# Conditioning vectors 2 to 8 from VectorE row products, and another ScalarE order in the first attention

## The chip, the cores and the metric

One core of a Trainium2 chip runs the whole program. The metric is the device time of one execution in microseconds. Engines are named as in the profile: PE is TensorE (PEld its weight loads), DVE VectorE, ACT ScalarE, POOL GpSimd, SP SyncE, which here only issues DMAs.

## What is computed

A conditioned block over 256 tokens of width 1024 with 256 context tokens (a feed-forward half, a token mixer with a long convolution and a differential attention, a second feed-forward half), followed by a second block with a recurrent mixer and a 16-expert layer. All is float32. The change concerns the nine conditioning vectors, for the token stream and the context stream, and the first attention:

```python
mod_x = split((silu(c)     @ w_ada + b_ada), 9)     # w_ada: 1024 x 9216
mod_c = split((silu(c_ctx) @ w_ada + b_ada), 9)
xs = ffn_half(xs, mod_x[0], mod_x[1], mod_x[2], g[0], g[1], w_ff_in, w_ff_out)   # shift, scale, gate
cs = ffn_half(cs, mod_c[0], mod_c[1], mod_c[2], g[0], g[1], w_ff_in, w_ff_out)
hx = modulate(rmsnorm(xs, g[2]), mod_x[3], mod_x[4])
hc = modulate(rmsnorm(cs, g[2]), mod_c[3], mod_c[4])
# mixer; xs += mod_x[5] * ...; second half uses mod_x[6], mod_x[7], mod_x[8]
# attention, for each of 8 heads and two maps m:
#   p = softmax(q k^T / 8);  p = p[0] - lam * p[1];  o = p @ v
```

## The kernel before

All activations lie transposed, features on the 128 partitions, tokens along the free axis. One SBUF tensor, `arena`, is cut by hand into 23 pages of 2048 words, whose use changes from stage to stage. Weights stream through four pages, the ring: SyncE loads slabs of 1 MB (16 blocks of 128x128) in the order in which TensorE uses them, a new one as soon as TensorE has started on the slab behind (`slab_started`). The order of the work on each engine is written out by hand; engines meet through semaphores, `full[b]` and `evac[b]` for the eight PSUM banks.

The conditioning vectors: `cond_s` holds silu of both conditioning vectors, two used columns in each 32. `ada_sums` (matmul at L768) multiplies one slab of `w_ada` (256 input rows by 1024 outputs) with them in four groups of 32 columns of the array, four slabs for each conditioning vector; VectorE copies the result (L1827), `ada_columns` (L782) turns it with four small matmuls, and VectorE adds the bias (L1832) into `mods`. Vectors 0 and 1 are made at the start (`ada_head`). Vectors 2 to 6 are made in ffn1_in, the first feed-forward product: its loop has 5 turns of 4 quarters, each with one slab of `w_ada` and then a pair of output tiles (gate and up, 8 products of 128x128 by 512 tokens each). ScalarE applies Silu to the gate tile (L1475), VectorE multiplies by the up tile (L1863). Vectors 7 and 8 are made between the tiles of z (24 tiles of 8 products by 256 tokens; ScalarE L1503, VectorE L1894 and L1896).

The start: ScalarE squares the tokens, takes the root (L1432), and issues 8 DMAs (L1447 to L1454). VectorE takes the reciprocal, then `normalise` (L1777, L1783) writes the input of ffn1_in, one of 8 feature tiles after the other, and TensorE's first product waits for each.

The end of ffn1_in: `filter_in_time` makes 8 tiles of the convolution filter on four banks (TensorE L818), VectorE multiplies them with the decay (L1855), ScalarE takes magnitudes (L1461), TensorE sums them (L825), and ffn1_out follows.

The first attention, for each head hd: TensorE makes the scores of the next head (L948, banks 0 to 3), part of another projection (L954), the transposes of this head's probabilities (L977, banks 5 and 6), more of L954, and the value product (L986, bank 7). VectorE takes maxima (L1953), normalises and mixes the two maps (L1961 to L1968), and copies bank 6 (L1974). ScalarE takes the exponentials of the next head from banks 0 to 3 (L1531), then copies bank 5 (L1538), then bank 7 (L1541).

Of the kernel before, what the change touches and what calls it, by code (L numbers as in the profile page):

```python
# [16 lines left out]
P = 128  # L17
D = 1024
T = 256
# [9 lines left out]
RING = 4  # L29
EX_RING = 16  # L30
# [24 lines left out]
DENSE = [("ffn1_in", FT + 20), ("ffn1_out", 11), ("z", 12 + 8), ("qk", 8), ("v", 4), ("gates", 8),  # L55
# [5 lines left out]
def _rot(n, banks=(0, 1, 2, 3)):  # L61
# [4 lines left out]
          ("ada_head", {7: 2, 6: 2}), ("ffn1_in", {0: 11, 1: 11, 2: 11, 3: 11, 7: 5, 6: 5}),  # L66
          ("w4", _rot(8)), ("knorm", {5: 1}), ("ffn1_out", _rot(8)),
          ("kdft", _rot(10)), ("z", {**_rot(24), 7: 2, 6: 2}), ("qk", {**_rot(16), 5: 8, 6: 8}), ("ut", {5: 2, 6: 2}), ("v", _rot(12)),
# [132 lines left out]
def cols(v):  # L201
    return v.reshape(-1, P).T
# [6 lines left out]
def lay_out(inp):  # L209
    g = {k: np.asarray(v) for k, v in inp.items()}  # L210
    ada = np.stack([k_pairs(g["w_ada"][0][:, m * D:m * D + D]) for m in range(N_MOD)])
# [6 lines left out]
    mixed = []  # L218
    for i in range(5):
        for q in range(4):  # L220
            mixed += [ada[2 + i][q:q + 1], slabs(f1[4 * i + q:4 * i + q + 1])]
    mixed += [slabs(f1[20:22])]
    w_in = g["w_in"][0]
    zs, late = slabs(blocks(w_in[:, :3 * D])), np.concatenate([ada[7], ada[8]])
    z = [a[i:i + 1] for i in range(12) for a in (zs, late) if i < len(a)]
# [12 lines left out]
        *mixed, slabs(blocks(g["w_ff_out"][0, 0])), *z, slabs(blocks(w_in[:, 3 * D:5 * D])),  # L238
# [12 lines left out]
    cond = np.stack([cols(g["c"][0]), cols(g["c_ctx"])], axis=2).reshape(P, KD * 2)  # L251

# [24 lines left out]
    out = {"ada_head": np.concatenate([ada[0], ada[1]]), "dense": dense, "experts": experts, "tokens": tokens, "cond": cond, "cols": cc, "filt": filt,  # L277
# [5 lines left out]
_ARRAYS = ["ada_head", "dense", "experts", "tokens", "cond", "cols", "filt", "w4", "lora", "router", "zT", "decay", "Fu", "FK", "FKalt",  # L283
# [4 lines left out]
def build(nc, dram, out_dram):  # L288
# [8 lines left out]
    with ctx:  # L297
# [19 lines left out]
        ring_flat = [page(i, SLAB) for i in range(RING)]  # L317
        head_flat = [page(i, SLAB) for i in (6, 7, 8, 9, 10, 11, 12, 14)]
# [17 lines left out]
        gain = sb("gain", [P, 4 * KD])  # L336
        filt = page(20, 3 * 64)[0:64]
# [162 lines left out]
        cond_ready = sem("cond_ready")  # L500
        sq_ready = sem("sq_ready")
# [216 lines left out]
        def _(pe):  # L718
# [30 lines left out]
            def tiles(stage, count, k_tiles, rhs, n=T, after=None, norm=None):  # L749

                for t in range(count):
# [3 lines left out]
                    if after:  # L755
                        after(t)

            def ada_sums(stage, k, kp):
# [4 lines left out]
                if head and kp == 0:  # L763
                    pe.wait_ge(head_in[k], 64)
# [1565 lines left out]
```

## Time and profile before

| | us |
|---|---|
| median of 3 runs | 2259.53 |
| lowest and highest | 2257.13, 2260.47 |
| the profiled execution | 2257.64 |
| its span | 2255.8 |
| TensorE busy in the span | 1975.7 |
| VectorE busy | 466.9 |
| ScalarE busy | 293.7 |
| TensorE's mean granted clock, share of full | 0.923 |

The page of the profile gives busy times by engine, the span in 40 slices, the chain of work that ended last, and the costliest groups of instructions. The trace behind it was asked for tables by stretch and for the instructions in order of time, one engine after the other, around each place that the change touches.

### The profile page before, as it was taken

How to read it: one execution, taken by the hardware profiler on the slowest of the kernel's cores; microseconds unless marked ns; L12 is line 12 of the kernel's file. 1: busy time of each engine (PE TensorE's matmuls, PEld its weight loads, DVE VectorE, ACT ScalarE, POOL GpSimd, SP SyncE). 2: the span in 40 equal slices, each digit the busy share in tenths (PEclk: the TensorE clock that was granted, in tenths of full speed). 3: DMA queues.
4: the chain of work that ended last, by engine and by line, in shares of the span. 5: the costliest groups of instructions: out<-in, count | busy, mean ns of one | idle time of the engine just before them, and what ended most of it. 6: DMA issues, size and time to landing. Idle time of an engine off the chain costs nothing.

```text
span 2255.8 us, 24413 instructions
## 1 busy us (share of the span) xinstructions
PE 1975.7 (88%) x10258; PEld 1253.2 (56%) x10258; DVE 466.9 (21%) x918; ACT 293.7 (13%) x590; POOL 37.7 (2%) x32
## 2 busy tenths in 40 slices
PE   5999999999999999989899989799999756565665
PEld 2444445444578478668688867688678512121212
DVE  4000001001422221351300023724142300000001
ACT  2000001001211001330110013312131100000001
POOL 0000000000000000000000000212000000000000
PEclk9999999999999999999899999889799887877878
DMA  9333331221263112203344423100034899999996
GB/s 365 118 143 149 142 121 72 75 75 56 89 247 131 67 64 94 94 38 131 139 157 149 149 101 123 57 3 3 19 112 160 338 422 421 422 421 422 421 422 253
DMA packets 55883, 393.95 MB, mean 175 GB/s; under 512 B 6355, under 2 KB 6708, under 8 KB 8892
## 3 DMA queue, kind: packets, MB, share of 16 engines
q1 hardware_dynamic: 54000, 384.29, 43.2%
q10 hardware_dynamic: 1804, 8.47, 1.0%
q8 instruction: 65, 1.06, 0.2%
q14 instruction: 14, 0.11, 0.0%
HBM read 391.69 MB, written 1.05 MB: 174 GB/s over the span
## 4 chain that ended last, share of the span: by engine, by line
PE 31%; DMA 17%; DVE 3%; issue 1%; SPq 1%; ACT 1%; POOL 0%; ACTq 0%; DVEq 0%; POOLq 0%
PE bank L729 20%; DMA arena<-experts_dram 17%; PE bank L1098 3%; PE bank L1340 2%; SPq L671 1%; PE bank L740 1%; PE bank L1167 1%; DVE arena L2106 1%; PE bank L1184 1%; PE bank L1182 1%; DVE rstd L1749 0%; PE bank L1170 0%; PE bank L1223 0%; PE bank L1270 0%; PE bank L1198 0%
## 5 line engine op out<-in xcount | busy, mean ns | idle before, releaser
L729 PE MATMUL bank<-arena 128*128 128x256 f32 (+1 forms) x4096 | 1168.1, 446 | 12.6 <-issue 5.0
L729 PEld LDWEIGHTS bank<-arena 128*128 128x128 f32 x4096 | 783.0, 192 | 392.3 <-issue 307.1
L1340 PE MATMUL bank<-arena 128*32 128x512 f32 x1536 | 246.9, 803 | 170.2 <-DMA arena<-experts_dram 170.2
L1340 PEld LDWEIGHTS bank<-arena 128*32 128x32 f32 x1536 | 66.2, 141 | 345.4 <-issue 345.3
L1863 DVE TENSOR_TENSOR arena<-sil,bank 128x512 f32 (+3 forms) x44 | 24.4, 555 | 445.7 <-PE bank L729 445.7
L1475 ACT ACTIVATE sil<-bank 128x512 f32<-128x512 f32 (+1 forms) x44 | 21.6, 491 | 413.8 <-PE bank L729 413.7
L1098 PE MATMUL bank<-arena 64*64 64x64 f32 x2048 | 65.9, 227 | 6.8 <-POOL arena L700 5.5
L1098 PEld LDWEIGHTS bank<-arena 64*64 64x64 f32 x2048 | 65.0, 143 | 8.1 <-POOL arena L700 5.8
L2290 DVE TENSOR_TENSOR arena<-arena,bank 128x512 f32<-128x512 f32 x8 | 5.5, 688 | 258.8 <-PE bank L1340 258.8
L910 PE MATMUL bank<-arena 128*128 128x256 f32 x256 | 55.6, 379 | 0.0
L910 PEld LDWEIGHTS bank<-arena 128*128 128x128 f32 x256 | 48.6, 190 | 7.0 <-issue 0.5
L1428 ACT ACTIVATE sq<-bank 128x256 f32<-128x256 f32 (+1 forms) x24 | 10.9, 455 | 296.5 <-PE bank L729 296.5
L740 PE MATMUL bank<-sq,small 128*128 128x256 f32 (+1 forms) x96 | 37.8, 541 | 10.4 <-ACT sq L1428 9.6
L1758 DVE TENSOR_TENSOR rstd<-rstd,sq 128x256 f32<-128x256 f32 (+1 forms) x18 | 9.3, 514 | 181.5 <-ACT sq L1428 181.5
L768 PE MATMUL bank<-arena,cond_s 128*32 128x512 f32 x288 | 40.0, 645 | 1.3 <-issue 1.3
L1719 ACT ACTIVATE arena<-bank 128x512 f32<-128x512 f32 x8 | 4.8, 597 | 234.6 <-PE bank L1340 234.6
L834 PE MATMUL bank<-arena 128*128 128x512 f32 x80 | 34.7, 592 | 0.0
L2129 DVE TENSOR_TENSOR arena<-arena,bank 128x512 f32<-128x512 f32 x40 | 27.5, 688 | 32.6 <-PE bank L1098 29.6
L740 PEld LDWEIGHTS bank<-sq,small 128*128 128x128 f32 x96 | 17.7, 221 | 29.4 <-ACT sq L1428 26.4
L1428 ACT ACTIVATE sq<-arena 128x256 f32<-128x256 f32 (+1 forms) x48 | 23.1, 487 | 80.7 <-PE bank L740 38.9
L2296 DVE COPY arena<-bank 128x512 f32<-128x512 f32 x4 | 2.8, 692 | 147.7 <-PE bank L1340 147.7
L954 PE MATMUL bank<-arena 128*128 128x256 f32 x128 | 33.2, 405 | 0.0
(310 smaller groups left out, 1311.4 us busy)
## 6 DMA issues: line engine op xcount, KB each, us to landing
arena<-experts_dram SPq DMA_DIRECT2D x189, 1024.0 KB, 22.7
arena<-dense_dram SPq DMA_DIRECT2D x165, 1024.0 KB, 4.8
arena<-ada_head_dram SPq DMA_DIRECT2D x8, 1024.0 KB, 18.4
arena<-experts_dram SPq DMA_DIRECT2D x6, 512.0 KB, 7.2
arena<-tokens_dram ACTq DMA_DIRECT2D x1, 2048.0 KB, 11.4
arena<-masks_dram ACTq DMA_DIRECT2D x1, 1184.0 KB, 5.9
arena<-decay_dram ACTq DMA_DIRECT2D x1, 1024.0 KB, 9.6
arena<-FK_dram ACTq DMA_DIRECT2D x1, 1024.0 KB, 10.2
```

The costliest lines, as they stand in the source:

```text
L671: sp.dma_start(ex_flat[j], slab).then_inc(ex_loaded[j], 16)
L729: ins = mm(out, lhsT=w, rhs=rhs(k), start=k == 0, stop=k == k_tiles - 1)
L740: mm(ps[4][:, 0:n], lhsT=ones, rhs=sq_v[:, j % 2, 0:n], start=j == 0, stop=j == 7)\
L768: ins = mm(ps[7][32 * q_:32 * q_ + 32, :], lhsT=cond_v[:, 2 * kp + par, :], rhs=slab[:, par * D + half * 512:par * D + half * 512 + 512], ...
L834: ins = mm(ps[n % 4][:, :], lhsT=part, rhs=hfil[:, kt, (n % 2) * 512:(n % 2) * 512 + 512], start=kt == 0, stop=kt == 3)
L910: ins = mm(ps[tt][:, 0:256], lhsT=h1[:, k, tt * P:tt * P + P], rhs=ring_wide[slot][:, k, :], start=k == 0, stop=k == KD - 1)
L954: ins = mm(ps[4][:, 0:T], lhsT=w, rhs=hy[:, k, :], start=k == 0, stop=k == KD - 1)
L1098: ins = mm(out[r64, H * hd:H * hd + H], lhsT=lhs[r64, 8 * d + hd, :], rhs=eye2[r64, :] if rhs is None else rhs[r64, 8 * d + hd, :], start= ...
L1340: ins = mm(ps[banks[half]][32 * e:32 * e + 32, :], lhsT=lhs[:, 2 * kp + par, CAP * e:CAP * e + CAP], rhs=slab[e][par][:, half * 512:half * ...
L1428: A(sq_v[:, j % 2, 0:n], src, ACT.Square).then_inc(sq_ready, 1)
L1863: tt_(hid[:, at, 0:n], sil_v[:, q_ % 2:q_ % 2 + 1, 0:n], ps[b + 1][:, 0:n].unsqueeze(1), mult)\
L2129: tt_(dst, dst, ps[b][:, :].rearrange("p (i n) -> p i n", n=H), sub).then_inc(evac[b], 1)
```

## The change

Only vectors 0 and 1 are still made by TensorE. For vectors 2 to 8, the weights are laid out transposed, as 56 tiles of 128 outputs (partitions) by 1024 inputs, 0.5 MB each, in a ring of five buffers of their own. Both conditioning vectors are loaded spread over all partitions (`cond_wide`, 128x2048, 1 MB) and go through one Silu on ScalarE. For each tile VectorE does two `scalar_tensor_tensor` with a sum along the free axis, one for each stream, into a column of `ada_acc`; after ten tiles it adds the bias into `mods`. The tiles are placed behind VectorE's gating products in ffn1_in, 2, 2, 3 and 3 in the quarters of a loop turn and three behind each of the last two. ScalarE issues the reloads, each after a wait for the tile that used the buffer. Its DMAs for `cond_wide` and the first five tiles stand ahead of the 8 that it issues at the start, and VectorE waits for the Silu before its first normalisation. Slabs of `w_ada` leave SyncE's stream in ffn1_in and z.

In the attention ScalarE takes the exponentials of banks 0 and 1 of the next head, copies bank 5, and then takes those of banks 2 and 3.

```diff
+ADA_TILES = (N_MOD - N_HEAD_MODS) * KD
+ADA_RING = 5
+ADA_SHARE = (2, 2, 3, 3)
...
+    ada_rest = w_ada[:, N_HEAD_MODS * D:].T.reshape(ADA_TILES, P, D)
+    cond_wide = np.broadcast_to(np.concatenate([g["c"][0], g["c_ctx"]])[None, :], (P, 2 * D))
...
+        ada_ring = [page(at, D) for at in (15, 15.5, 21, 21.5, 18)]
+        cond_wide = page(20, 2 * D)
...
                 with pe.Fori(0, 5) as i:
-                    st.loop(i, per)
+                    st.loop(i, 4)
                     for q_ in range(4):
-                        if with_ada:
-                            ada_sums(stage + "_in", i, q_)
                         pair(q_, i * 2 + q_ // 2)
-                    if with_ada:
-                        ada_columns(stage + "_in", i, i)
...
-            tiles("z", 24, KD, lambda k: h1[:, k, 0:T], T, late_ada, 1)
+            tiles("z", 24, KD, lambda k: h1[:, k, 0:T], T, norm=1)
...
             root(0, 512)
+            act.dma_start(cond_wide, dram["cond_wide"]).then_inc(cond_wide_in, 16)
+            for s in range(ADA_RING):
+                act.dma_start(ada_ring[s], dram["ada_rest"][s]).then_inc(ada_in[s], 16)
             act.dma_start(w4[0:64, :], dram["w4"]).then_inc(decay_in, 16)
...
                 with act.Fori(0, 5) as i:
                     for q_ in range(4):
                         gate(q_, i * 2 + q_ // 2)
+                        if ada:
+                            for t in range(sum(ADA_SHARE[:q_]), sum(ADA_SHARE[:q_ + 1])):
+                                act.wait_ge(ada_used, i * 11 + (t + 2))
+                                act.dma_start(ada_ring[t % ADA_RING],
+                                              dram["ada_rest"][ds(i * 10 + (t + ADA_RING), 1), :, :].rearrange("s p n -> (s p) n"))\
+                                    .then_inc(ada_in[t % ADA_RING], 16)
...
+            act.wait_ge(cond_wide_in, 16)
+            A(cond_wide, cond_wide, ACT.Silu).then_inc(cond_wide_ready, 1)
+            ffn("ffn1", 1, y1, 512, magnitudes, ada=True)
...
-            exps(0)
+            exps(0, range(4))
             for hd in range(HEADS):
                 if hd + 1 < HEADS:
-                    exps(hd + 1)
+                    exps(hd + 1, range(2))
                 got(act, "att", 5, hd)
                 A(pT[:, 4 * (hd % 2):4 * (hd % 2) + 4, 0:P], ps[5][:, :].rearrange("p (k n) -> p k n", n=P), ACT.Copy)\
                     .then_inc(evac[5], 1)
+                if hd + 1 < HEADS:
+                    exps(hd + 1, range(2, 4))
...
+            dve.wait_ge(cond_wide_ready, 1)
+            V.memset(ada_acc[:, :], 0.0).then_inc(ada_used, 1)
             normalise(X, h1, [(0, T, gain_v[:, 0, :], mod(0, 0)), (T, 2 * T, gain_v[:, 1, :], mod(0, 1))])
...
+                def ada_tile(t, i):
+                    w = ada_ring[t % ADA_RING]
+                    dve.wait_ge(ada_in[t % ADA_RING], i * 32 + 16 * (t // ADA_RING + 1))
+                    dve.wait_ge(ada_used, i * 11 + (t + 1))
+                    stt(sq[:, :], w, 1.0, cond_wide[:, 0:D], mult, mult, accum_out=ada_acc[:, 2 * t:2 * t + 1])
+                    stt(w, w, 1.0, cond_wide[:, D:2 * D], mult, mult, accum_out=ada_acc[:, 2 * t + 1:2 * t + 2])                        .then_inc(ada_used, 1)
...
-                        if with_ada and q_ == 3:
-                            ada_sums(stage + "_in", i)
                         up(q_, i * 2 + q_ // 2, ds(i * 4 + q_, 1))
+                        if with_ada:
+                            for t in range(sum(ADA_SHARE[:q_]), sum(ADA_SHARE[:q_ + 1])):
+                                ada_tile(t, i)
...
+                for q_ in range(2):
+                    up(q_, 10, slice(20 + q_, 21 + q_))
+                    if with_ada:
+                        for t in range(3 * q_, 3 * q_ + 3):
+                            ada_tile(t, 5)
```

## Rows read from the trace of the kernel before

**Rows 1.** The page: busy time by engine, and the chain's engines.
```profile
PE 1975.7 (88%) x10258; PEld 1253.2 (56%) x10258; DVE 466.9 (21%) x918; ACT 293.7 (13%) x590; POOL 37.7 (2%) x32
...
PE 31%; DMA 17%; DVE 3%; issue 1%; SPq 1%; ACT 1%; POOL 0%; ACTq 0%; DVEq 0%; POOLq 0%
```
**Rows 2.** Busy time by stretch: PE, PEld, DVE, ACT, POOL, clock, DMA share, GB/s.
```profile
1750.00:2000.00 250.00, 161.62 (x995) 69.01 (x994) 28.61 (x65) 16.87 (x29) 0.00 (x0) 0.80 0.97 403
```
**Rows 3.** In order of time, ffn1_in: start, duration, engine, line, operation.
```profile
63.60 1.06 PE L768 MATMUL bank<-arena,cond_s 128*32 128x512 f32 x8
...
336.96 0.19 PEld L729 LDWEIGHTS bank<-arena 128*128 128x128 f32 x1 [0.24 <-issue]
...
349.40 0.19 PEld L729 LDWEIGHTS bank<-arena 128*128 128x128 f32 x1 [0.24 <-issue]
...
378.71 7.13 PE L818 MATMUL bank<-arena,fh 64*128 64x512 f32 x16
```
**Rows 4.** In order of time, z: TensorE's first and nineteenth tile, ScalarE at one.
```profile
597.95 7.07 PE L729 MATMUL bank<-arena 128*128 128x256 f32 x32
...
671.36 23.99 PE L729 MATMUL bank<-arena 128*128 128x256 f32 x110
...
682.01 0.56 ACT L1503 ACTIVATE arena<-bank,col_sb 128x256 f32<-128x256 f32 x1 [2.89 <-PE bank L729]
```
**Rows 5.** VectorE's groups by form (count, busy us, mean ns), and an accumulator read.
```profile
L1968 DVE SCALAR_TENSOR_TENSOR arena<-arena,tiny 128x512 f32<-128x512 f32 x16 | 11.3, 748 | 0.3
...
L2045 DVE TENSOR_TENSOR arena<-arena 128x1024 f32<-128x1024 f32 x2 | 2.5, 1226 | 0.1
...
1782.64 0.07 DVE L2251 DVE_READ_ACCUMULATOR sq<-fh,sil 16x1 f32 x1
```
**Rows 6.** The start in order of time; clock by stretch; a DMA to landing; a group.
```profile
6.45 9.29 SPq L639 DMA_DIRECT2D arena<-dense_dram  x4
...
36.99 0.48 ACTq L1447 DMA_DIRECT2D arena<-w_dram  x1
...
43.27 1.28 ACT L1475 ACT_TABLE_LOAD   x1 [4.36 <-issue]
...
44.66 0.49 DVE L1777 SCALAR_TENSOR_TENSOR arena<-arena,gain,rstd 128x256 f32<-128x256 f32 x1
...
50.00:51.00 1.00, 1.00 (x2) 0.50 1.04 395
...
arena<-decay_dram ACTq DMA_DIRECT2D x1, 1024.0 KB, 9.6
...
L1697 ACT ACTIVATE arena<-arena 128x2048 f32<-128x2048 f32 x2 | 3.7, 1902 | 0.0
```
**Rows 7.** The end of ffn1_in in order of time, and the clock by stretch.
```profile
378.89 0.69 DVE L1863 TENSOR_TENSOR arena<-sil,bank 128x512 f32<-128x512 f32 x1 [13.04 <-PE bank L729]
379.94 1.48 DVE L1855 TENSOR_TENSOR arena<-bank,arena 128x512 f32<-128x512 f32 x2 [0.36 <-PE bank L818]
...
387.29 12.29 PE L825 MATMUL bank<-small,arena 128*128 128x1 f32 x64 [1.45 <-ACT arena L1461]
...
390.00:392.00 2.00, 2.00 (x11) 2.00 (x11) 0.00 (x0) 0.00 (x0) 0.00 (x0) 0.50 0.00 0
```
**Rows 8.** The first attention in order of time, VectorE, ScalarE and TensorE.
```profile
943.83 2.50 DVE L1953 TENSOR_REDUCE tiny<-bank 128x1 f32<-128x512 f32 x4
...
949.49 0.18 DVE L1961 RECIPROCAL tiny<-tiny 128x4 f32<-128x4 f32 x1
...
952.98 0.69 DVE L1953 TENSOR_REDUCE tiny<-bank 128x1 f32<-128x512 f32 x1 [0.82 <-PE bank L948]
...
949.90 1.99 PE L986 MATMUL bank<-arena 128*128 128x256 f32 x8 [0.96 <-ACT arena L1538]
...
955.97 0.69 ACT L1531 ACTIVATE arena<-bank,tiny 128x512 f32<-128x512 f32 x1 [3.20 <-DVE tiny L1955]
...
959.29 1.99 PE L986 MATMUL bank<-arena 128*128 128x256 f32 x8 [0.96 <-ACT arena L1538]
```

More of the change, by code:

```diff
@@ L52 @@
 N_COLS = _at
-DENSE = [("ffn1_in", FT + 20), ("ffn1_out", 11), ("z", 12 + 8), ("qk", 8), ("v", 4), ("gates", 8),
+DENSE = [("ffn1_in", FT), ("ffn1_out", 11), ("z", 12), ("qk", 8), ("v", 4), ("gates", 8),
          ("hyout", 4), ("daout", 4), ("wo", 4), ("ffn2_in", FT), ("ffn2_out", 11), ("rwkv", 18.5 + 8)]
@@ L210, in lay_out @@
     g = {k: np.asarray(v) for k, v in inp.items()}
-    ada = np.stack([k_pairs(g["w_ada"][0][:, m * D:m * D + D]) for m in range(N_MOD)])
+    w_ada = g["w_ada"][0]
+    ada = np.concatenate([k_pairs(w_ada[:, m * D:m * D + D]) for m in range(N_HEAD_MODS)])
+    ada_rest = w_ada[:, N_HEAD_MODS * D:].T.reshape(ADA_TILES, P, D)
     def ffn_in(w):
@@ L280, in lay_out @@
     return {k: np.ascontiguousarray(v) for k, v in out.items()}
-_ARRAYS = ["ada_head", "dense", "experts", "tokens", "cond", "cols", "filt", "w4", "lora", "router", "zT", "decay", "Fu", "FK", "FKalt",
+_ARRAYS = ["ada_head", "ada_rest", "cond_wide", "dense", "experts", "tokens", "cond", "cols", "filt", "w4", "lora", "router", "zT", "decay", "Fu", "FK", "FKalt",
            "Finv", "rope", "small", "headbc", "masks"]
@@ L500, in build @@
         cond_ready = sem("cond_ready")
+        cond_wide_in = sem("cond_wide_in")
+        cond_wide_ready = sem("cond_wide_ready")
+        ada_in = [sem(f"ada_in{i}") for i in range(ADA_RING)]
+        ada_used = sem("ada_used")
         sq_ready = sem("sq_ready")
@@ L747, in stat_of_sum, with tiles @@
                 mm(ps[4][:, 0:n], lhsT=ones, rhs=rstd[:, 0:n], start=True, stop=True).then_inc(full[4], 1)
-            def tiles(stage, count, k_tiles, rhs, n=T, after=None, norm=None):
+            def tiles(stage, count, k_tiles, rhs, n=T, norm=None):
                 for t in range(count):
@@ L761, in ada_sums @@
                     take(pe, stage, 7, k)
-                head = stage == "ada_head"
-                if head and kp == 0:
+                if kp == 0:
                     pe.wait_ge(head_in[k], 64)
-                slab = head_flat[4 * k + kp] if head else st.whole(ring_flat)
+                slab = head_flat[4 * k + kp]
                 for q_ in range(4):
@@ L770, in ada_sums @@
                              start=kp == 0, stop=kp == KD // 2 - 1)
-                    if q_ == 0 and not head:
-                        ins.then_inc(slab_started, 1)
                 if kp == KD // 2 - 1:
@@ L836, in filter_spectrum, with ffn @@
                     ins.then_inc(full[n % 4], 1)
-            def ffn(stage, r, src, hid, n, with_ada, norm, between=None):
+            def ffn(stage, r, src, hid, n, norm, between=None):
                 def pair(q_, use):
@@ L1467, in filter_spectrum, with ffn @@
                         .then_inc(evac[n % 4], 1)
-            def ffn(stage, r, y, n, between=None):
+            def ffn(stage, r, y, n, between=None, ada=False):
                 def gate(q_, use):
@@ L1880, in _ @@
             V.reciprocal(tiny[:, 8:16], tiny[:, 8:16]).then_inc(kn_ready, 1)
-            evacuated(dve, "ffn1_in", 6, 4)
+            dve.wait_ge(ada_used, 63)
             for r in range(2):
```

56 lines of the change are left out of this document (24 added, 32 removed).

## The prediction

> **What bounds the kernel now.** I began with the page's busy times and its chain [rows 1]. The reader is to see a TensorE at work for 88% of the span, and a chain that consists of TensorE and, at the end, of expert loads. The table by stretches shows where each limit holds: the last 500 us move 403 GB/s with TensorE at 161.6 of 250 us [rows 2], so there loads set the pace. They are only issued behind events of the stages before them, so what those stages gain shifts the whole tail forward and is kept. Before 1000 us TensorE is the limit nearly everywhere, above all in the first feed-forward block and in the z projection, and TensorE work removed there counts in full. Three places are different: the start, where VectorE's normalisation releases TensorE; the filter made in time at the end of ffn1_in, where VectorE, ScalarE and TensorE take turns; and the first attention, where a loop of VectorE, ScalarE and TensorE turns more slowly than TensorE's own work.
>
> **Part 1: TensorE loses 28 conditioning slabs and 7 transpositions.**
> In ffn1_in the slab of quarter (0, 1) starts at 63.60, and the stage's successor (L818) starts at 378.71 [rows 3]: 315.1 us for 21 pairs of tiles, 19 slabs and 5 groups of L782. A pair is 32 weight loads (16 products, two records each). Between 336.96 and 349.40 there are 29 steps of load to load [rows 3], 0.429 us each, so a pair alone is 13.73 us and 21 pairs are 288.3. The difference is 26.8 us; the twentieth slab, at 44 us, fills a hole in which TensorE waits for VectorE anyway and gives nothing. VectorE sat idle for 13 us between two gating products here (its idle time before L1863 [rows 7]), and ScalarE likewise, so nothing else is late next: **-26.8**.
> In z, the first tile starts at 597.95 and the nineteenth at 671.36 [rows 4]: 73.4 us for 18 tiles, 8 slabs, 2 groups of L782. ScalarE's step at each tile (0.56 busy, 2.89 idle) shows a tile alone at 3.45 us [rows 4]; 18 are 62.1. VectorE's two or three steps of 0.5 us fit under that, so TensorE stays the limit. **-11.3**.
> The bytes of weights are the same as before. They move from SyncE's queue, at 1 MB, to ScalarE's, at 0.5 MB, and those of z now come in ffn1_in: 50 MB in some 300 us, 170 GB/s, against the 403 that the tail shows [rows 2]. A tile's next load is asked for five tiles before its use, some 27 us. I cost this at nothing.
>
> **Part 2: the row products on VectorE.** 56 tiles, two scalar-tensor-tensor with sum each, of 128x1024. The nearest rows: the same instruction on 512 elements from SBUF takes 0.748 us (two in a row 1.41), a plain tensor-tensor of 1024 takes 1.226, and an accumulator read is 0.07 [rows 5]. So 1.23 + 0.07 = 1.3 each, 2.6 a tile, 146 us in all; bounds are 1.23 and 1.50 (twice the 0.748) + 0.07 each. I take 1.3, since two rows at a distance of a factor of two agree on one element per cycle. A quarter with three tiles is 7.9 us and the gating product 0.7, against 13.7 us of TensorE work: hidden. ScalarE now waits for those tiles before it issues their reloads, and its next Silu is queued behind; it comes about 9.4 us after the last one instead of 6.9, but the bank that it frees is wanted only at 13.7. Hidden too.
> The Trainium skill (Vector Engine (DVE) Microarchitecture Reference, Points that are easy to get wrong) says that this very instruction halves its throughput when both sources are SBUF tensors other than bf16, which is what the change uses. The trace's 0.748 us for 512 such elements [rows 5] is not half speed beside 1.226 for 1024 of a tensor-tensor, so the row speaks against it; the row has no accumulator, though, and I keep the case as a rival.
>
> **Part 3: the start.** VectorE now waits, before its first normalisation, for ScalarE's Silu over the broadcast conditioning vector. Ahead of that Silu on ScalarE's queue are now 14 DMA issues instead of 8. The 8 begin at 36.99 and the table load behind them at 43.27 [rows 6]: 0.78 each. Six more at this mean are 4.7 us, so the table load starts at 48.0. Then 1.28 for it and 1.90 for 2048 elements (the same length at L1697 [rows 6]): 51.1. The load of 1 MB itself was issued first and should be down by 46 or so: the decay, issued second at the same place and of the same size, took 9.6 us [rows 6] behind 0.5 MB. VectorE's first step moves from 44.66 [rows 6] to about 51.2 with the memset: 6.5 us later, and TensorE with it. Bounds: 0.48 an issue, as the first of them [rows 6], +4.7; or a queue that is held as SyncE's was, four issues in 9.29 us [rows 6], for the last four, +13. TensorE's granted clock was at half (0.50, 1.2 GHz) until 51 [rows 6], after it had stood and waited for VectorE; now it stands longer and will again be at half when the products begin, with VectorE's pace of 1.31 us a product hiding most of it. I add 0.5: **+7.0**.
>
> **Part 4: the end of ffn1_in.** VectorE has three tiles and a bias left after its last gating product, before it takes over filter tiles. Now: gating product at 378.89, filter products from 379.94, column sums of the magnitudes at 387.29 [rows 7]. New, with T = 378.71: gating product done at T + 0.9, tiles until T + 8.8, bias T + 9.1. TensorE has filled four banks by T + 3.5 and stands for 6.4 us. Then the other four at 0.86 us each as now: column sums from T + 14.9 instead of T + 8.6, +6.3. But a stop of 1.45 us already ends in a half clock here (0.50 in 390 to 392 [rows 7]), and 6.4 us of idling will do so earlier: the four matmuls at 1.71 instead of 0.86 add 3.4, and the first sums, now still at full clock, 0.7. **+10.4**, with bounds +6.3 (no fall of the clock) and +14 (the half clock reaches on into ffn1_out).
>
> **Part 5: ScalarE's order in the attention.** In the steady state a head takes 9.40 us (TensorE's L986 waits for ScalarE's copy and starts at 959.29, as at 949.90) [rows 8]. VectorE starts at 949.49, its reductions start only at 952.98, after 0.82 us of waiting for scores (so it was done with the rest at 952.16, 2.67 later); ScalarE's exponentials start at 955.97, the copy of bank 5 behind them is what the value product waits for [rows 8]. Four exponentials and a copy of 0.6 thus fill the 3.3 us from 955.97 to 959.29, 0.67 an exponential. With the new order the copy stands between the second and third exponential: the copy and with it the value product and the next scores come 1.3 us sooner, the last exponentials 0.6 later. The loop is then VectorE 2.67, four reductions back to back 2.50 (as at 943.83 [rows 8]), 0.25, four exponentials and the copy 3.3, and 0.2: about 8.95 instead of 9.40. Over 5 such heads that is 2.2; the change costs 0.6 once at the first of them and saves 1.6 behind the last, where the transposes come sooner. **-3.2**, bounds 0 (the loop closes over another engine at 9.4) and -4.5.
>
> **Sum:** -26.8 - 11.3 - 3.2 + 7.0 + 10.4 = -23.9. The profiled execution took 2257.64 us (span 2255.8), so 2233.7; the median of the runs is 2259.53, so about 2235.5. I say 2235.
>
> **Rivals.**
> (a) *The sum makes a row product twice as long* as the tensor-tensor of the same size: 2.46 and the read, 5.0 a tile. Ten tiles and four gatings are 53 us against 54.9 of a loop turn, so the loop stays hidden, but a quarter with three tiles takes 15.7 against 13.7 and VectorE comes about 6 us late to the last gating product; then three tiles take 15 instead of 7.9. Together 13 more: 2248. For it: no row here has a sum over 1024 elements and two tensors. Against: the accumulator read of 0.07 and the 0.748 [rows 5]. This is the case that the page's rule above describes.
> (b) *ScalarE's queue is held at the start*: +13 instead of +7, 2241. For it: SyncE's four issues at 2.3 us each behind 11 others [rows 6], and ScalarE's own mean of 0.78 against 0.48 for its first. Against: SyncE's eight before them were short.
> (c) *The clock doesn't fall in the new hole, or the start is cheaper than I hold*: 2229.
> (d) *VectorE becomes the bound of ffn1_in*. A loop turn of TensorE is 54.9; VectorE needs 10 tiles and 3.0. It decides above 5.19 us a tile. Beyond that each microsecond of a tile costs 50 + 3 us, and the whole change turns to a loss at 5.5 us a tile; with 6 us (3 us an instruction) it gives about 2286. For it: 112 long instructions put on one engine, with DMA-filled buffers. Against: it wants over twice the longest of rows 5.
> (e) *The change doesn't do what it says*: reloads by ScalarE arrive late, since each is queued behind gatings and waits for VectorE, and VectorE stands at an empty buffer with the gating queued behind it. It has 27 us for half the size of a transfer that took 9.6 among full queues [rows 6]; at 5 us in each loop turn the gain would be gone: 2260.
>
> **How the numbers follow.** Forecast 0.60, for which its own range is 2229 to 2242; (a) 0.10, (b) 0.12, (c) 0.12, (d) 0.02, (e) 0.04. The range of 8 in 10 takes in (a), (b) and (c) with the bounds of parts 3 to 5: down to 2228 (start +4.7, end +6.3, attention -4.5) and up to 2248 (start +13, end +14, attention 0), the lower end widened by 2 us for what separates executions of one kernel (2257.1 to 2260.5). Within 0.2% (4.5 us), about what a measurement can tell from no change, means over 2255; only (e) in a milder form reaches that: same 0.03. Slower is (d) and the worst of (e): 0.03. Faster 0.94.
>
> **What would show each step.** Right: no gap for slabs in L729's run in ffn1_in, a pair each 13.7 us; the VectorE instruction at 1.3 us; the first normalisation at 51; a hole of 6 us in L818 and the clock at 0.50 behind it; heads at 8.95. Wrong: VectorE idle on ada_rest loads; pairs longer than 13.8; the Silu of 2048 after 54; the clock at full through L818; heads still at 9.4. The prediction as a whole is wrong if TensorE waits for a bank inside ffn1_in.

## The result, and the profile of the changed kernel

| | before | changed |
|---|---|---|
| median of 4 runs, us | 2259.46 | 2226.84 |
| lowest and highest | 2257.13, 2260.47 | 2225.04, 2228.48 |
| the profiled execution | 2257.64 | 2228.48 |
| its span | 2255.8 | 2226.7 |
| TensorE's mean granted clock | 0.923 | 0.919 |

The ratio is 0.9857, with an interval of 0.984 to 0.9874: 32.6 us less in the medians, 29.1 less in the two spans. 2235 was forecast, with 2226 to 2248 as the range. The two differences are not the same because the profiled execution of the changed kernel lies 1.6 above its median, and that of the kernel before 1.8 below its own.

The changed kernel's page, busy times, and from its list of groups and of DMA issues the new work (count, busy us, mean ns; for a DMA, size and us to landing); the first line answers to [rows 1]:

```profile
PE 1939.1 (87%) x9978; PEld 1244.4 (56%) x9978; DVE 592.0 (27%) x1135; ACT 290.4 (13%) x587; POOL 37.7 (2%) x32
...
L1877 DVE SCALAR_TENSOR_TENSOR sq<-arena 128x1024 f32<-128x1024 f32 x56 | 68.4, 1222 | 1.5
L1878 DVE SCALAR_TENSOR_TENSOR arena<-arena 128x1024 f32<-128x1024 f32 x56 | 68.3, 1220 | 0.0
...
arena<-ada_rest_dram ACTq DMA_DIRECT2D x56, 512.0 KB, 3.7
```

TensorE has 280 matmul records fewer (each product leaves two), VectorE 125 us more work. A row product takes 1.22 us.

The start in order of time (start, duration, engine, line, operation, idle before and what ended it), which answers to [rows 6]:

```profile
35.55 0.33 ACTq L1437 DMA_DIRECT2D arena<-cond_wide_dram  x1
...
44.96 1.11 ACTq L1447 DMA_DIRECT2D router<-router_dram  x1
46.10 1.28 ACT L1496 ACT_TABLE_LOAD   x1 [8.62 <-issue]
47.39 1.91 ACT L1496 ACTIVATE arena<-arena 128x2048 f32<-128x2048 f32 x1
49.36 0.46 DVE L1783 SCALAR_TENSOR_TENSOR arena<-arena,gain,rstd 128x256 f32<-128x256 f32 x1 [5.91 <-issue]
...
51.78 7.52 PE L736 MATMUL bank<-arena 128*128 128x512 f32 x12 [8.82 <-DVE arena L1789]
```

The Silu stands behind 14 DMA issues and its table load, and VectorE behind the Silu for 5.91 us.

The end of ffn1_in, in order of time and by stretch (TensorE busy, granted clock, DMA share, GB/s), which answers to [rows 3] and [rows 7]:

```profile
356.67 3.70 PE L820 MATMUL bank<-arena,fh 64*128 64x512 f32 x8
356.85 0.69 DVE L1871 TENSOR_TENSOR arena<-sil,bank 128x512 f32<-128x512 f32 x1 [5.79 <-PE bank L736]
357.45 1.22 DVE L1877 SCALAR_TENSOR_TENSOR sq<-arena 128x1024 f32<-128x1024 f32 x1
358.60 0.08 DVE L1877 DVE_READ_ACCUMULATOR sq<-arena 128x1 f32 x1
...
364.92 2.48 DVE L1863 TENSOR_TENSOR arena<-bank,arena 128x512 f32<-128x512 f32 x4
...
365.65 7.19 PE L820 MATMUL bank<-arena,fh 64*128 64x512 f32 x8 [5.29 <-DVE arena L1863]
...
374.29 11.04 PE L827 MATMUL bank<-small,arena 128*128 128x1 f32 x51 [1.44 <-ACT arena L1454]
...
362.00:364.00 2.00, 0.00 (x0) 0.78 0.00 0
364.00:366.00 2.00, 0.34 (x1) 0.50 0.00 0
...
388.00:392.00 4.00, 4.00 (x6) 0.50 0.19 33
```

Here T of the prediction is 356.67. TensorE fills its banks in 3.70 us, stands 5.29 us until VectorE is through the three tiles behind its last gating product, and does the other half at half clock (granted 0.50, 1.2 GHz), which still holds at 392.

The first attention, the value products of two heads in a row, which answers to [rows 8]:

```profile
943.34 0.59 ACT L1542 ACTIVATE arena<-bank 128x512 f32<-128x512 f32 x1
943.99 1.99 PE L976 MATMUL bank<-arena 128*128 128x256 f32 x8 [0.27 <-ACT arena L1542]
...
952.70 1.99 PE L976 MATMUL bank<-arena 128*128 128x256 f32 x8 [0.27 <-ACT arena L1542]
```

A head now takes 952.70 - 943.99 = 8.71 us, before 9.40.

**Where the 29.1 us come from**, by the starts of TensorE's stages in the two traces (of the start, VectorE's first normalisation):

| stretch | before | changed | difference | forecast |
|---|---|---|---|---|
| until the first normalisation | 44.66 | 49.36 | +4.7 | +7.0, with the clock |
| from there to the first filter product | 334.05 | 307.31 | -26.7 | -26.8 |
| to the column sums | 8.58 | 17.62 | +9.0 | +9.7 |
| to the start of z | 210.66 | 213.51 | +2.9 | +0.7 |
| z, to the first scores | 325.93 | 314.59 | -11.3 | -11.3 |
| attention, to the sums behind its heads | 81.97 | 76.91 | -5.1 | -3.2 |
| everything behind it | 1249.95 | 1247.4 | -2.6 | 0 |
| sum | | | -29.1 | -23.9 |

### The profile page after: what moved, and what is told of

Its sections match the earlier page's. It is cut to its first block, busy times and chain, and to the rows that moved or that the text cites. A ratio compares the mean times of both kernels' runs of the same rounds, so it can differ in the third digit from the quotient of the medians.

```text
span 2226.7 us, 24201 instructions
## 1 busy us (share of the span) xinstructions
PE 1939.1 (87%) x9978; PEld 1244.4 (56%) x9978; DVE 592.0 (27%) x1135; ACT 290.4 (13%) x587; POOL 37.7 (2%) x32
## 4 chain that ended last, share of the span: by engine, by line
PE 31%; DMA 17%; DVE 3%; issue 1%; ACT 1%; SPq 1%; POOL 0%; ACTq 0%; DVEq 0%; POOLq 0%
PE bank L736 21%; DMA arena<-experts_dram 17%; PE bank L1088 3%; PE bank L1330 2%; SPq L678 1%; PE bank L747 1%; PE bank L1157 1%; DVE arena L2130 1%; PE bank L1174 1%; PE bank L1172 1%; DVE rstd L1755 0%; PE bank L1160 0%; PE bank L1213 0%; PE bank L1260 0%; PE bank L1188 0%
## 5 line engine op out<-in xcount | busy, mean ns | idle before, releaser
L1330 PE MATMUL bank<-arena 128*32 128x512 f32 x1536 | 247.1, 804 | 170.2 <-DMA arena<-experts_dram 170.2
L1330 PEld LDWEIGHTS bank<-arena 128*32 128x32 f32 x1536 | 66.3, 141 | 344.9 <-issue 344.8
L1088 PE MATMUL bank<-arena 64*64 64x64 f32 x2048 | 66.0, 227 | 6.7 <-POOL arena L707 5.5
L1088 PEld LDWEIGHTS bank<-arena 64*64 64x64 f32 x2048 | 65.2, 143 | 8.1 <-POOL arena L707 5.8
L1877 DVE SCALAR_TENSOR_TENSOR sq<-arena 128x1024 f32<-128x1024 f32 x56 | 68.4, 1222 | 1.5
L1878 DVE SCALAR_TENSOR_TENSOR arena<-arena 128x1024 f32<-128x1024 f32 x56 | 68.3, 1220 | 0.0
L900 PE MATMUL bank<-arena 128*128 128x256 f32 x256 | 55.6, 379 | 0.0
L747 PE MATMUL bank<-sq,small 128*128 128x256 f32 (+1 forms) x96 | 37.5, 535 | 10.4 <-ACT sq L1418 9.6
L1977 DVE TENSOR_REDUCE tiny<-bank 128x1 f32<-128x512 f32 x32 | 19.9, 680 | 53.1 <-PE bank L938 53.1
## 6 DMA issues: line engine op xcount, KB each, us to landing
arena<-tokens_dram ACTq DMA_DIRECT2D x1, 2048.0 KB, 12.2
```

The lines of the kernel that those rows point to most:

```text
L747: mm(ps[4][:, 0:n], lhsT=ones, rhs=sq_v[:, j % 2, 0:n], start=j == 0, stop=j == 7)\
L900: ins = mm(ps[tt][:, 0:256], lhsT=h1[:, k, tt * P:tt * P + P], rhs=ring_wide[slot][:, k, :], start=k == 0, stop=k == KD - 1)
L1088: ins = mm(out[r64, H * hd:H * hd + H], lhsT=lhs[r64, 8 * d + hd, :], rhs=eye2[r64, :] if rhs is None else rhs[r64, 8 * d + hd, :], start= ...
L1330: ins = mm(ps[banks[half]][32 * e:32 * e + 32, :], lhsT=lhs[:, 2 * kp + par, CAP * e:CAP * e + CAP], rhs=slab[e][par][:, half * 512:half * ...
L1877: stt(sq[:, :], w, 1.0, cond_wide[:, 0:D], mult, mult, accum_out=ada_acc[:, 2 * t:2 * t + 1])
L1878: stt(w, w, 1.0, cond_wide[:, D:2 * D], mult, mult, accum_out=ada_acc[:, 2 * t + 1:2 * t + 2]) .then_inc(ada_used, 1)
```

## The experiments

The table shows what differs, not that the causes add up as I read them. My theory, A, is that the start, the hole at the end of ffn1_in and the attention each have the price or gain that the table shows, one by one and in sum, and that the row products themselves and their 28 MB of loads are hidden. The rival, B, stands in each expectation: in the main, that a gain would be given back later, or that the row products cost something even where no gap shows them. All ratios are to the kernel before, run on the same chip.

### The wait for the Silu put behind the normalisation

```diff
-            dve.wait_ge(cond_wide_ready, 1)
-            V.memset(ada_acc[:, :], 0.0).then_inc(ada_used, 1)
             normalise(X, h1, ...)
+            dve.wait_ge(cond_wide_ready, 1)
+            V.memset(ada_acc[:, :], 0.0).then_inc(ada_used, 1)
```

> The changed kernel (2226.8 us) with VectorE's wait for the Silu and the memset moved behind the first normalisation; nothing is left out. Theory A: the wait is what moved the first normalisation from 43.4 (gain ready) to 49.36, so it starts at 43.5, TensorE's first product likewise 5.9 us sooner, and the kernel takes about 2221. Theory B: TensorE is at half clock there and the DMA engines are full, so most of the 6 us is lost again in the first products: 2225 or more.

2224.04 us (five runs, 2218.57 to 2227.73), ratio 0.9852 (0.9838 to 0.9866), span 2216.7. In order of time, the start, the end of ffn1_in and z:

```profile
44.01 1.67 DVE L1783 SCALAR_TENSOR_TENSOR arena<-arena,gain,rstd 128x256 f32<-128x256 f32 x4
...
46.45 7.55 PE L736 MATMUL bank<-arena 128*128 128x512 f32 x12 [2.97 <-DVE arena L1789]
...
582.57 77.65 PE L736 MATMUL bank<-arena 128*128 128x256 f32 x359
```

The first product is 5.3 us earlier than the changed kernel's 51.78, and z as much (582.57 against 587.80): nothing of it is given back in the first 580 us. But the medians differ by 2.8 us only, and this kernel's runs lie 9 us apart, into the changed kernel's. Its median lies between the 2221 of A and the 2225 of B, so by time alone this run doesn't tell one from the other; the third experiment does.

### The last six tiles ahead of the last gating product

```diff
-for q_ in range(2):
-    up(q_, 10, slice(20 + q_, 21 + q_))
-    for t in range(3 * q_, 3 * q_ + 3):
-        ada_tile(t, 5)
+for t in range(2):
+    ada_tile(t, 5)
+up(0, 10, slice(20, 21))
+for t in range(2, 6):
+    ada_tile(t, 5)
+up(1, 10, slice(21, 22))
```

Two tiles now come ahead of the gating product (0, 10), and the other four behind it, so that none is left behind the last one.

> The changed kernel with the last six tiles placed two before the gating product of pair 20 and four behind it, none behind that of pair 21; nothing is left out. Theory A: the three tiles behind the last gating product make the hole of 5.3 us in L820 and with it the early half clock; both go, the column sums start 8.6 us behind L820 instead of 17.6 and ffn1_out loses the 2.8 us that it gained in length: 12 less, 2215. Theory B: only VectorE's share of the hole goes (6.3 us) and the granted clock falls as early as it does now: 2220.

2214.64 us (2213.21 to 2218.82), ratio 0.9807 (0.9793 to 0.982), span 2217.0: 12.2 us less than the changed kernel. TensorE in order of time:

```profile
356.48 7.13 PE L820 MATMUL bank<-arena,fh 64*128 64x512 f32 x16
...
365.05 11.91 PE L827 MATMUL bank<-small,arena 128*128 128x1 f32 x64 [1.44 <-ACT arena L1454]
...
575.74 84.55 PE L736 MATMUL bank<-arena 128*128 128x256 f32 x391
```

The eight filter products (16 records) are one run of 7.13 us again, as in [rows 3], and the column sums come 8.57 us behind its start (before 8.58, changed 17.62). z starts 12.1 us sooner than in the changed kernel: 9.0 for the hole and the four products at half clock, 2.8 for the half clock that reaches on behind it (column sums to z 210.7 against 213.5), 0.2 from before it. So the order of six tiles is worth 12 us in this comparison, more than the 10.4 of my sum; the next experiment gives a second one, and it is smaller.

### Both

> Both moves together. Theory A: the two places are far apart and add up: 2226.8 - 5.9 - 11.9 = 2209. Theory B: they share something (the clock, the loads): over 2212.

2209.83 us (2208.83 to 2212.36), ratio 0.979 (0.9776 to 0.9803), span 2208.0. It leaves nothing out and is the fastest version that was run, 17.0 us below the changed kernel (14.8 below its repetition, further down). Against the second experiment, in the same batch, the later wait gives 4.8 us, where A says 5.9, with ranges that don't touch (2208.83 to 2212.36 against 2213.21 to 2218.82): the start's price is real, and the runs of the first experiment were too scattered to show it. The column sums:

```profile
359.45 13.72 PE L827 MATMUL bank<-small,arena 128*128 128x1 f32 x64 [1.45 <-ACT arena L1454]
```

The two places are not quite independent, and what B names, the clock, is what they share. There is no hole here, and yet the column sums take 13.72 us, at half clock from their start (0.53 in the first 2 us, then 0.50) and as long as behind the hole (13.81 in full), where the tiles early alone had 11.91 and the kernel before 12.29. So the filter products start 5.6 us sooner than with the tiles early alone, but z only 4.0. Measured against the kernel with the later wait, the tiles' order brings z forward by 10.8 us, of which 0.5 come from before the filter products: 10.3, and not 12.

### No row products at all

This kernel leaves out the conditioning vectors 2 to 8 (they are zero): no loads of their weights or of `cond_wide`, no Silu over it, no tiles.

```diff
-act.dma_start(cond_wide, dram["cond_wide"]).then_inc(cond_wide_in, 16)
-for s in range(ADA_RING):
-    act.dma_start(ada_ring[s], dram["ada_rest"][s]).then_inc(ada_in[s], 16)
...
-dve.wait_ge(cond_wide_ready, 1)
-V.memset(ada_acc[:, :], 0.0).then_inc(ada_used, 1)
+V.memset(mods[:, 4 * KD:], 0.0).then_inc(ada_used, 1)
...
-ffn_in("ffn1", hid1, 512, True)
+ffn_in("ffn1", hid1, 512, False)
```

> The changed kernel without the row products, their loads, the wide Silu and the waits: vectors 2 to 8 are zeros, so that part of the computation is left out. It shows what the row products cost wherever they lie. Theory A: all that they cost is the start (5.9) and the end of ffn1_in (11.9), so this takes 2209, the same as both moves together within 2 us. Theory B: the 137 us of VectorE work and 28 MB of loads in ffn1_in also slow TensorE's products or loads while hidden: clearly below 2206, and below both moves together.

2209.21 us (2208.25 to 2217.75), ratio 0.9793 (0.9776 to 0.981), span 2207.5. Its filter products and z, and behind the dots the same two lines of the kernel with both edits:

```profile
351.04 7.13 PE L820 MATMUL bank<-arena,fh 64*128 64x512 f32 x16
...
571.61 88.66 PE L736 MATMUL bank<-arena 128*128 128x256 f32 x410
```

```profile
350.88 7.13 PE L820 MATMUL bank<-arena,fh 64*128 64x512 f32 x16
...
571.75 88.44 PE L736 MATMUL bank<-arena 128*128 128x256 f32 x409
```

They agree within 0.2 us at both places, and the medians within 0.6. So 137 us of VectorE work and 28 MB of loads cost nothing that can be measured, once the wait at the start and the tail are out of the way. What the change pays, some 15 us against its repetition and 17 against its first runs, is paid at those two places.

### The attention's order alone

```diff
-def exps(hd):
+def exps(hd, banks):
-    for b in range(4):
+    for b in banks:
...
-    exps(hd + 1)
+    exps(hd + 1, range(2))
...
+if hd + 1 < HEADS:
+    exps(hd + 1, range(2, 4))
```

> The kernel before with ScalarE's new order in the attention and nothing else changed. Theory A, from the trace of the changed kernel (heads at 8.71 us, 5.05 less between the first scores and the head sums): 5 less than before, 2252 to 2254, ratio 0.9978. Theory B, the sum of the prediction: 3.2 less, ratio 0.9986. Theory C: part of the 5 us came from the clock's phase, which the other edits shifted: 0 to 2 less.

On the kernel before, with nothing else changed: 2252.95 us (2249.63 to 2257.34), ratio 0.998 (0.9971 to 0.9989), span 2252.0; the kernel before had 2257.2 beside it. TensorE in order of time, a value product and the sums behind the heads:

```profile
982.55 1.99 PE L986 MATMUL bank<-arena 128*128 128x256 f32 x8 [0.28 <-ACT arena L1538]
...
991.26 1.99 PE L986 MATMUL bank<-arena 128*128 128x256 f32 x8 [0.27 <-ACT arena L1538]
...
1000.45 3.62 PE L993 MATMUL bank<-arena,small 128*8 128x256 f32 x16 [0.92 <-ACT arena L1545]
```

The heads are 8.71 us here too. From the first scores (922.75) to the sums are 77.70 us, where before had 81.97: 4.3 us, and 4.3 in the medians. The new order is worth 4.3 here, more than my 3.2. In the ten traces that have the other edits too the same stretch takes 75.8 to 76.9 us, up to 1.9 less than here; what makes that difference was not taken apart.

### Each row product done twice

```diff
 stt(sq[:, :], w, 1.0, cond_wide[:, 0:D], ...)
+stt(sq[:, :], w, 1.0, cond_wide[:, 0:D], ...)
+stt(sq[:, :], w, 1.0, cond_wide[:, D:2 * D], ...)
 stt(w, w, 1.0, cond_wide[:, D:2 * D], ...)
```

A wait of VectorE's for itself stands between two of them. This is rival (a)'s tile, made real: the prediction said that the loop would stay hidden up to 5.19 us a tile.

> The changed kernel with each row product made twice, each waiting for the one before; results are the same. It doubles the hidden work. Theory A: a tile takes 5.2 us; a quarter with three tiles then needs 16.3 us against 13.7, VectorE comes some 7 us late to the last gating product and spends 8 more behind it, while within the loop TensorE never waits for a bank: 15 to 16 more, 2243. Theory B: the cover is thinner than thought, TensorE waits for banks in each loop turn: over 2260. Theory C: VectorE's work is no part of the price: 2227.

2258.09 us (2255.65 to 2265.86), ratio 1.0005 (0.9997 to 1.0014), span 2257.3: the whole gain is gone, 15 us more than A had said and a little under B's 2260. VectorE in ffn1_in in order of time, two gating products with two tiles between them, and the first row product of each tile:

```profile
189.07 0.69 DVE L1872 TENSOR_TENSOR arena<-sil,bank 128x512 f32 x1 [1.31 <-ACT sil L1469]
189.68 1.22 DVE L1878 SCALAR_TENSOR_TENSOR sq<-arena 128x1024 f32<-128x1024 f32 x1
...
194.74 1.23 DVE L1878 SCALAR_TENSOR_TENSOR sq<-arena 128x1024 f32<-128x1024 f32 x1
...
201.15 0.69 DVE L1872 TENSOR_TENSOR arena<-sil,bank 128x512 f32 x1 [1.38 <-ACT sil L1469]
```

and ScalarE's Silu in the same quarter of two turns:

```profile
170.80 0.60 ACT L1469 ACTIVATE sil<-bank 128x512 f32<-128x512 f32 x1 [16.54 <-DVE arena L1884]
...
229.76 0.60 ACT L1469 ACTIVATE sil<-bank 128x512 f32<-128x512 f32 x1 [16.55 <-DVE arena L1884]
```

A tile takes 194.74 - 189.68 = 5.06 us, less than 5.19, and yet VectorE and ScalarE take 59.0 us for a turn where TensorE needs 54.9. After each quarter's tiles VectorE waits 1.3 to 1.4 us for ScalarE: the Silu that its next gating product wants is queued behind ScalarE's waits for those very tiles, and can start only when VectorE is through. Each quarter thus has a part in which neither works beside the other: 10 x 5.06 + 4 x (0.61 + 1.4) + 0.3 = 58.9. By the same terms, as an estimate that no run tests, the loop decides from (54.9 - 0.3 - 4 x 2.0) / 10 = 4.66 us a tile, not from 5.19.

TensorE itself first stands for a Silu at 247.91, for 1.65 us, and then at 306.86, for 3.50. Up to there it keeps its own pace, since the pairs alternate between two sets of banks, so that the other two engines can fall behind by more than a pair: the Silu that it waits for at 247.91 comes, by TensorE's pace, some 21 us after its tile was done. So the lag of 4 us a turn grows unseen for most of the loop and comes due at its end. Theory B had the right wait, though not in each turn.

### The Silu a quarter ahead, with products done twice and once

If ScalarE's place in its queue is the cause, taking each Silu before the waits must give the loop back, and do nothing where each product is done once.

```diff
+gate(0, 0)
...
-gate(q_, i * 2 + q_ // 2)
+nxt = q_ + 1
+gate(nxt % 4, i * 2 + nxt // 2)
...
-gate(0, 10)
```

> The kernel with doubled row products, with one more edit: ScalarE takes its Silu one quarter ahead of the reloads (first Silu before the loop, in the loop the Silu of the next quarter and then the waits and reloads of this one); results are the same. Theory A: the doubled kernel lost 33 us because ScalarE's Silu stands behind its waits for the row products, so that a quarter is VectorE's tiles, then Silu, then gating, in a row (VectorE idle 1.4 us in each, 59.4 us a loop turn); with the Silu ahead a turn is 10 tiles of 5.07 and four gatings, 53.7, under TensorE's 54.9, and only the lateness at the last gating (6.6) and the longer tail (7.6) stay: 2225 + 14 = 2239. Theory B: VectorE's work alone made it: 2255 or more.

> The changed kernel itself with that edit of ScalarE's order alone; results are the same. At single row products TensorE doesn't wait in the loop, so both theories say no change within 2 us: 2225 to 2227. Less than 2222 would mean that the coupling costs something in the changed kernel too.

Products twice: 2238.83 us (2238.02 to 2244.46), ratio 0.9923 (0.9901 to 0.9946). Products once: 2228.44 (2226.15 to 2232.16), ratio 0.9871 (0.9849 to 0.9892), a little over the 2225 to 2227 expected and no better than the changed kernel; its column sums start at 373.98, between the 374.29 and 373.43 of the changed kernel's two traces. With the products doubled, ScalarE in the loop and TensorE at the end of ffn1_in:

```profile
170.66 0.60 ACT L1469 ACTIVATE sil<-bank 128x512 f32<-128x512 f32 x1 [13.14 <-PE bank L737]
...
184.39 0.60 ACT L1469 ACTIVATE sil<-bank 128x512 f32<-128x512 f32 x1 [13.14 <-PE bank L737]
```

```profile
355.95 2.84 PE L821 MATMUL bank<-arena,fh 64*128 64x512 f32 x6
363.60 2.07 PE L821 MATMUL bank<-arena,fh 64*128 64x512 f32 x2 [4.81 <-DVE arena L1879]
379.63 7.19 PE L821 MATMUL bank<-arena,fh 64*128 64x512 f32 x8 [13.96 <-DVE arena L1871]
388.27 4.00 PE L828 MATMUL bank<-small,arena 128*128 128x1 f32 x18 [1.45 <-ACT arena L1455]
```

The Silu is ended by TensorE's product again and comes every 13.73 us, TensorE's own pace; the filter products start at 355.95, no later than with single products (356.36). The loop stays hidden at the 5.06 us a tile that bound it before: of the 33 us that doubling cost (2258.09 against 2224.64 for the changed kernel beside it), some 19 (2258.09 - 2238.83) were the order of ScalarE's queue, or 21 by what each stands from the kernel before beside it. What is left is at the tail. VectorE comes late to its last gating product and then has three tiles of 5 us: column sums 32.3 us behind the first filter product, against 17.6, 14.7 more. In the medians that is 10.4 more (2238.83 - 2228.44). Rival (a) had priced just this at 13, so its arithmetic for the tail holds once the loop is free, but in the changed kernel's own order it would have cost 33.

The coupling is there with single products too, and costs nothing. ScalarE's Silu behind a quarter of three tiles, in the changed kernel:

```profile
214.33 0.60 ACT L1468 ACTIVATE sil<-bank 128x512 f32<-128x512 f32 x1 [14.88 <-DVE arena L1878]
```

It is ended by the last of three tiles and comes 15.5 us after the Silu before it instead of 13.73, but TensorE doesn't wait for it.

### The Silu at the head of ScalarE's queue

```diff
 act.dma_start(cond_wide, dram["cond_wide"]).then_inc(cond_wide_in, 16)
+act.wait_ge(cond_wide_in, 16)
+A(cond_wide, cond_wide, ACT.Silu).then_inc(cond_wide_ready, 1)
 for s in range(ADA_RING):
     ...
-act.wait_ge(cond_wide_in, 16)
-A(cond_wide, cond_wide, ACT.Silu).then_inc(cond_wide_ready, 1)
```

> The changed kernel with the wide Silu directly behind its own load's issue, ahead of the other 13 issues on ScalarE's queue; nothing is left out. Theory A: the 13 issues ahead of the Silu set its time; now only the load (8.9 us, landed at 44.4) does, the Silu runs from 44.5 to 46.4 and the first normalisation starts at 46.5 instead of 49.4: 3 less, 2224, and the filter's loads, issued later, are still early enough for 350. Theory B: those loads come late or the queue of issues hurts elsewhere: 2227 or more.

2221.39 us (2220.77 to 2226.5), ratio 0.9849 (0.9836 to 0.9862), span 2219.6. The start in order of time:

```profile
43.71 1.91 ACT L1439 ACTIVATE arena<-arena 128x2048 f32<-128x2048 f32 x1 [4.58 <-DMA arena<-cond_wide_dram]
...
45.68 0.46 DVE L1783 SCALAR_TENSOR_TENSOR arena<-arena,gain,rstd 128x256 f32<-128x256 f32 x1 [2.13 <-issue]
...
48.10 12.48 PE L736 MATMUL bank<-arena 128*128 128x512 f32 x22 [5.05 <-DVE arena L1789]
```

The Silu waits for its load and for nothing else, and the normalisation comes at 45.68 instead of 49.36. So the 13 DMA issues between the load and the Silu, with the table load of 1.28 us behind them that now lies under the wait for the load, set the start, for 3.7 us of it (2.8 against the repetition below, whose own start came sooner; 3.3 in the medians). The load itself, down at 43.7, is the rest: with the wait put later the normalisation stands at 44.01, another 1.7 us sooner.

### The changed kernel again

> The changed kernel itself, once more and beside the next three on one chip: 2227 again, within 2 us, if its spread is that of single executions.

2224.64 us (2223.26 to 2225.72), ratio 0.986 (0.9846 to 0.9875), 2.4 below the 2227 expected, so a little outside the 2 us that I allowed. The span is 2221.4, 5.3 us less than the first profiled execution of the same program. At the first 64x64 product (L1088) the two traces stand 1.3 us apart (1424.52 and 1423.25), at the first expert product (L1330) 6.5 (1763.85 and 1757.31). TensorE's busy time and granted clock, DMA share and GB/s in two stretches of 20 us, the first 40 us behind that 64x64 product, in the first trace and in this one:

```profile
1464.52:1484.52 20.00, 20.00 (x116) 0.53 0.00 1
1484.52:1504.52 20.00, 17.05 (x224) 0.93 0.01 2
```

```profile
1463.25:1483.25 20.00, 20.00 (x197) 0.74 0.01 2
1483.25:1503.25 20.00, 16.60 (x213) 0.90 0.01 2
```

At the same place in the program one execution is granted 0.53 and the other 0.74. The stretch to the first expert product takes 339.3 us in one and 334.1 in the other. Eleven of the twelve traces have one of the two lengths: 339 to 340 in before, changed, the attention alone, the tiles early and the Silu ahead with single products; 334 in the repetition, the later wait, both edits, no products, the Silu first and the Silu ahead with doubled products. Doubled products alone have 337. Of the 5 us between the two lengths, 1.2 are given back behind the first expert product. That is how one execution of a kernel can be 4 to 5 us from another. It may also be why the first experiment's runs, 2218.57 to 2227.73, wouldn't say what its trace said: the traced execution, with 334, was the fastest of them; the others left no trace.

## Why the prediction was right, point by point

**Part 1** held to 0.1 us in both stages: -26.7 against -26.8 and -11.3 against -11.3. Reading a pair's price from load to load in the run of before, and subtracting it from the whole stretch, was sound, and so was giving the twentieth slab nothing.

**Part 2** held. 1.22 us and a read of 0.08 that overlaps the next step, against 1.30; a tile 2.4 to 2.5 against 2.6; ScalarE's Silu behind three tiles 8.4 us after the gating product against 9.4; hidden, as the run without products shows. The rule of the Trainium skill (Vector Engine (DVE) Microarchitecture Reference, Points that are easy to get wrong), that this instruction loses half its throughput with two sources in SBUF other than bf16, does not show beside a plain tensor-tensor: 128x1024 float32 with a sum takes 1.222 us, and the tensor-tensor of that size 1.226 in [rows 5].

**Part 3** was right in kind and 2.3 us too dear: +4.7 instead of +7.0. The issues took what I gave them (10.55 us from 35.55 to 46.10, 0.75 each against 0.78), but the first began 1.4 us sooner than in the kernel before, which the change does not touch and which moves everything behind it; in the twelve traces that first issue lies between 34.9 and 37.0, and the kernel before has the latest of all. The 0.5 for the clock can't be found in the trace: from the normalisation to the first product are 2.42 us, before 2.31. The change's own price is better read from the kernel with the later wait: 51.78 - 46.45 = 5.3 at the first product. The kernel with the attention alone, whose start is that of before, has its first product at 45.80 and makes it 6.0. So 1.0 to 1.7 of the 2.3 were too dear, and the rest goes with that early start.

**Part 4** was right in its mechanism: 5.29 us of idling (I had said 6.4, with a tile at 2.6), the half clock behind it, four products at 1.71 us each. +9.0 to the column sums against +9.7. The failed term is the one behind them, 0.7 for the first sums, where 2.9 were lost: 1.5 in the column sums (from their start to ffn1_out 13.67 us, before 12.15) and 1.3 in ffn1_out, where the half clock holds to past 392. Only the 1.3 are the hole's for certain, since the kernels with both edits and without products have no hole and lose the 1.5 in the sums all the same; why the clock falls earlier in them than in the kernel before is open. Undoing the whole place gives 12.2 us in one comparison and 10.3 in the other, against 10.4 forecast.

**Part 5** was too small a gain: -5.1 in the trace, 4.3 alone, against -3.2. The failed term is the head's 8.95, which measured 8.71. From VectorE's first step of a head to ScalarE's first exponential are 5.31 us, where I had 2.67 + 2.50 + 0.25 = 5.42, and 3.40 from there, through four exponentials and a copy, to VectorE's next head, where I had 3.3 + 0.2; both gaps were put too wide. Five heads make 1.2 of the missing 1.9, and so all of what is missing in the kernel with the attention alone; the rest was not taken apart.

**Not in my sum:** 2.6 us behind the attention, where nothing was changed. They are not the 5 us of the repeated run, since from the 64x64 products to the first expert product both traces of the table take 339 us. They lie before that, between the sums behind the heads and the first 64x64 product: 448.1 us before, 445.2 changed, but 447.0 in the changed kernel's repetition. In the 10 us that begin 80 us behind those sums TensorE was granted 0.84 in the changed kernel's first trace, in that with the later wait and in that with the Silu ahead and doubled products, the three in which this stretch takes 444.4 to 445.2; it was granted 0.67 in the other nine, with 446.9 to 449.6. So the 2.6 go with the clock, which one unchanged program was granted in both ways. That they are a difference between executions and not the change's is argued and not shown: no experiment holds the clock still.

So 2.3 too dear at the start, 1.5 too cheap at the end of ffn1_in, 1.9 too little for the attention and 2.6 that the change need not have made are the 5.2 us between -23.9 and -29.1. In the medians the gain is 32.6, another 3.5 that the two traces don't show. The direction and the range came out, the range narrowly: the measured time lies 0.8 us above its lower end, which had been widened by 2 us for the spread of executions, and it lies below the forecast's own 2229 to 2242. That it fell inside is in part luck.

**The rivals.** (c), a start cheaper than I hold, came nearest in time (2229), with the clock falling all the same. (b), a queue held at the start, did not come: no issue of ScalarE's at the start took over 1.53 us in the changed kernel's trace, and 2.62 was the longest in any. (e), late reloads, did not: a tile's load lands 3.7 us after its issue. (a) and (d) did not come either, but the threshold of 5.19 us a tile that both rest on was wrong. I had counted VectorE's work in a turn against TensorE's and left out that ScalarE's waits chain the two. Doubled products put the loop past its limit at 5.06 us a tile, and cost 33 us where (a) said 13. Had a row product really been twice as long, rival (a)'s 2248 would have been some 10 us too low by the measured 2258, and 20 by the 33 put on the forecast.

## What to carry to other kernels

Work moved to an idle engine was free inside the loop here, as long as it fitted under the other engine's, and paid for at the edges: look for what that engine must do first when the loop begins, and for what is left in its queue when the next stage's first step wants it. Six tiles in another order and one wait put later were worth 15 to 17 us here, about half as much as the whole change brought.

When an engine waits for another before it issues a reload, and its next real step is queued behind, the two form a chain; the loop's limit is then the sum of both, not the larger of them, and a reserve computed from busy times alone is too large. Buffers between the engines can hide the lag for several turns, so look for it at the end of the loop.

## What the runs showed of the hardware

- A `scalar_tensor_tensor` over 128x1024 float32, both sources in SBUF, with a sum along the free axis, takes 1.22 us, and its accumulator read 0.08, with 1.15 us from the start of one product to its read. The sum adds nothing that matters.
- ScalarE's DMA issues at the start take 0.33 to 1.53 us each in the changed kernel, and the compute instruction behind them waits for all of them: 10.55 us for 14.
- TensorE's idling of 5.29 us, in which the granted clock falls, is followed by 0.50 from 364 to about 393. A stop of 1.45 us alone is followed by 0.50 as well, but not at the same point: 2 us into the column sums in the kernel before, at their very start in the kernels with both edits and without products.
- One program, unchanged, is granted 0.53 or 0.74 over the same 20 us of its work and takes 334 or 339 us for the same stretch.
